# Cached keys loaded in small pieces and turned by VectorE, with ring slots of their own

## What is computed

```python
def sample_layer(x, c_fk, c_fv, c_logf, c_ckv, c_krope, c_mk, c_mv, p):   # x (8, 16, 1024)
    h = rmsnorm(x, p['g_mix'])
    fq, fk, fv, logf, q_lat, q_rope, ckv, krope, g_a, g_b = mixer_inputs(h, qpos, p)
    k_all = jnp.concatenate([c_fk, fk], axis=1)        # c_fk (8, 512, 8 heads, 64)
    v_all = jnp.concatenate([c_fv, fv], axis=1)
    ...
    fox_o = fox_attend(fq, k_all, v_all, cum[:, past:], cum, qpos, kpos)
    ckv_all = jnp.concatenate([c_ckv, ckv], axis=1)    # c_ckv (8, 512, 256), the latents
    ...
    mla_lat = mla_attend(q_lat, q_rope, ckv_all, krope_all, qpos, kpos)
    mix = mixer_output(fox_o, mla_lat, g_a, g_b, p)
    return residual_tail(x, mix, c_mk, c_mv, p), ...   # c_mk (8, 256, 4 heads, 128)

def fox_attend(q, k, v, cum_q, cum_k, qpos, kpos):
    s = jnp.einsum('bqhd,bkhd->bhqk', q, k) * FOX_SCALE
    ...                                                # forget-gate bias, mask, softmax, values

def cross_attend(h, mk, mv, p):
    q = (h @ p['w_xq']).reshape(B, T, X_HEADS, X_HEAD_DIM)
    s = jnp.einsum('bthd,bmhd->bhtm', q, mk) * X_SCALE
    ...                                                # softmax, values, w_xo

def residual_tail(x, mix, mk, mv, p):
    x = x + mix
    x = x + cross_attend(rmsnorm(x, p['g_x']), mk, mv, p)
    return x + moe(rmsnorm(x, p['g_ffn']), p)          # 32 experts, 4 per token
```

## Time and profile before

| | |
|---|---|
| median of 3 runs | 1525.36 us (1524.87 to 1526.36) |
| the profiled execution | 1524.94 us, of which the span from the first to the last instruction is 1523.1 us |
| TensorE busy | 1466.7 us, 96% of the span |
| VectorE, ScalarE busy | 552.6 us, 36%; 313.2 us, 21% |
| read from memory | 475.16 MB, 315 GB/s over the span |
| sample loop, about | 176 to 285 us |
| cross attention with memory loop, about | 502 to 568 us |
| experts, from about | 584 us |

### The profile page before, as it was taken

The page is one execution under the profiler, slowest core; times in us unless marked ns, Lnnn a source line. Parts: engine busy times, 40 slices in busy tenths (PEclk is TensorE's granted clock), DMA queues, the critical chain, the costliest instruction groups (busy, mean ns, idle before and its releaser), DMA issues.

```text
span 1523.1 us, 21869 instructions
## 1 busy us (share of the span) xinstructions
PE 1466.7 (96%) x8246; PEld 720.5 (47%) x8247; DVE 552.6 (36%) x1240; ACT 313.2 (21%) x676; POOL 45.4 (3%) x55
## 2 busy tenths in 40 slices
PE   8999899999999998999999999999999999999996
PEld 7766577655687653333333333333333333333332
DVE  4245444110302365333343333343333433333334
ACT  1225555210001441111111111111111111111111
POOL 0000000160000000000000000000000000000000
PEclk9999999999999998999999999999999999999998
DMA  9411466942332468999999999999999999999994
GB/s 287 131 67 47 116 184 215 304 156 86 111 125 83 153 259 360 427 427 429 428 428 429 430 428 428 428 430 389 431 428 428 429 429 429 428 429 429 429 428 199
DMA packets 83037, 483.48 MB, mean 317 GB/s; under 512 B 18144, under 2 KB 46080, under 8 KB 56368
## 3 DMA queue, kind: packets, MB, share of 16 engines
q1 hardware_dynamic: 68800, 471.78, 75.7%
q0 software_dynamic: 3168, 9.11, 2.6%
q10 hardware_dynamic: 11024, 1.96, 0.8%
HBM read 475.16 MB, written 4.65 MB: 315 GB/s over the span
## 4 chain that ended last, share of the span: by engine, by line
PE 79%; DMA 16%; DVE 2%; ACT 1%; issue 1%; SPq 0%; DVEq 0%; ACTq 0%
PE bank L529 74%; DMA ring<-in_w_gu 16%; PE bank L1283 1%; PE bank L683 1%; PE bank L1203 1%; DMA ring<-in_w_in 1%; PE bank L920 0%; PE bank L806 0%; PE bank L694 0%; PE bank L1066 0%; DVE small L1666 0%; PE bank L543 0%; DVE ring L1677 0%; PE bank L961 0%; DVE xr L1987 0%
## 5 line engine op out<-in xcount | busy, mean ns | idle before, releaser
L529 PE MATMUL bank<-ring,hT 128*64 128x512 f32 (+3 forms) x3648 | 814.1, 567 | 14.8 <-DMA ring<-in_w_gu 13.9
L529 PEld LDWEIGHTS bank<-ring,hT 128*64 128x64 f32 (+1 forms) x3648 | 305.6, 145 | 438.7 <-issue 387.8
L1945 DVE SCALAR_TENSOR_TENSOR xr<-bank,probTs,xr 128x512 f32<-128x512 f32 x198 | 139.2, 745 | 231.1 <-PE bank L529 231.1
L529 PE MATMUL bank<-hT,ring 128*128 128x384 f32 x384 | 124.4, 487 | 0.0
L2334 ACT ACTIVATE probTs<-hT 128x512 f32<-128x512 f32 x33 | 20.8, 629 | 412.4 <-DVE hT L1964 412.4
L1982 DVE TENSOR_TENSOR mlaT<-bank,foxT 128x512 f32<-128x512 f32 x33 | 22.8, 692 | 224.6 <-ACT foxT L2340 224.6
L529 PEld LDWEIGHTS bank<-hT,ring 128*128 128x128 f32 x384 | 72.9, 190 | 50.2 <-issue 0.2
L529 PE MATMUL bank<-ring 128*128 128x256 f32 (+7 forms) x434 | 84.9, 396 | 3.8 <-issue 2.5
L529 PE MATMUL bank<-foxT 64*128 64x512 bf16 x600 | 82.2, 380 | 0.8 <-ACT foxT L2340 0.8
L529 PEld LDWEIGHTS bank<-ring 128*128 128x128 f32 (+3 forms) x434 | 59.0, 171 | 20.0 <-issue 11.5
L2340 ACT CAST foxT<-bank 128x512 bf16<-128x512 f32 x33 | 19.3, 585 | 215.7 <-PE bank L529 215.7
(11 more groups left out here) (330 smaller groups left out, 1270.8 us busy)
## 6 DMA issues: line engine op xcount, KB each, us to landing
ring<-in_w_gu SPq DMA_DIRECT2D x128, 2048.0 KB, 24.1
ring<-in_w_down SPq DMA_DIRECT2D x64, 2048.0 KB, 26.5
ring<-in_w_in SPq DMA_DIRECT2D x16, 1024.0 KB, 11.5
ring<-in_cache_fox_k SPq DMA_DIRECT2D x8, 1024.0 KB, 4.8
ring<-in_cache_fox_v SPq DMA_DIRECT2D x8, 1024.0 KB, 7.7
ring<-in_cache_mla_ckv SPq DMA_DIRECT2D x8, 512.0 KB, 5.6
ring<-in_w_out SPq DMA_DIRECT2D x4, 1024.0 KB, 5.1
ring<-in_cache_mem_k SPq DMA_DIRECT2D x8, 512.0 KB, 3.2
```

The source lines that it names most:

```text
L529: return pe.matmul(o, l, r, start=start, stop=stop, skip_group_check=True)
L1945: v.scalar_tensor_tensor(x, sums[i % 2][:, :], gate_e[:, i // 2, e], x, ALU.mult, ALU.add).then_inc(shares_added, 1)
```

## The change

Fox keys of the batches in `FINE` (0, 1, 2, 3, 4 and 6) and all memory keys are loaded so that a 32x32 block transpose on VectorE finishes the turn. A row of keys is cut into pieces of 32 floats (128 bytes), and blocks of 32 tokens are laid on the 32 partitions where their channels will stand: 16 DMAs per fox key tile, each of 512 pieces, and 16 per memory tile, each of 256, plus one for the values, whose tokens are laid out in another order to match. VectorE waits for the tile and turns it from slot to `skT` in four transposes of 128x512 (`keys_in`), or to `xkT` in one of 128x1024 (`mem_out`). For batch 0 the four stand in the rounds i = 3 to 6 of the prompt's units (`KEYS_AT`), instead of two copies in round 7. TensorE's transposes and the copies out of banks on both engines go away for these tiles; batches 5 and 7 stay as they were. TensorE's first transposes of latents move ahead of the values in a step.

The ring's slots are shared out: two for fox keys, two for values, four for latents, by the batch's number, and the order of the stream is written anew. A slot with fine keys is released when VectorE has turned them (`keys_turned`).

```diff
+FINE = (0, 1, 2, 3, 4, 6)
...
-        for b in range(NB):
-            tile(("sk", b), whole(KT, FW, d["cache_fox_k"][0, b].rearrange("(p k) h n -> p k (h n)", k=KT)))
+        def key_tile(b):
+            if b not in FINE:
...
+            src = d["cache_fox_k"][0, b].rearrange("(i r) (g e) (f c) -> g e f r i c", r=32, e=2, c=32)
+            parts = []
+            for g in range(4):
+                for j in range(4):
+                    parts.append((lambda s, g=g, j=j: ring[32 * j:32 * j + 32, s, FW * g:FW * g + FW].rearrange("p (i c) -> p i c", c=32),
+                                  src[g, j // 2, j % 2, :, :, :]))
+            tile(("sk", b), parts)
...
+        for b in range(2):
+            key_tile(b)
+        for b in range(2):
+            latent_tile(b)
+        value_tile(0)
+        latent_tile(2)
+        key_tile(2)
+        latent_tile(3)
+        value_tile(1)
+        for b in range(NB - 2):
+            if b + 3 < NB:
+                key_tile(b + 3)
+            value_tile(b + 2)
+            if b + 4 < NB:
+                latent_tile(b + 4)
...
-            tile(("cm", b), [(lambda s: kview(s, 2, FW), d["cache_mem_k"][0, b].rearrange("(p k) h n -> p k (h n)", k=2)),
...
+            src = d["cache_mem_k"][0, b].rearrange("(i r) h (j c) -> h j r i c", r=32, c=32)
+            parts = []
+            for h in range(XH):
+                for j in range(4):
+                    parts.append((lambda s, h=h, j=j: ring[32 * j:32 * j + 32, s, MEM * h:MEM * h + MEM].rearrange("p (i c) -> p i c", c=32),
+                                  src[h, j, :, :, :]))
+            parts.append((lambda s: ring[:, s, 1024:2048].rearrange("p (k n) -> p k n", k=2),
+                          d["cache_mem_v"][0, b].rearrange("(k p) h n -> p k (h n)", k=2)))
+            tile(("cm", b), parts)
...
+        fl = place["fl"]
+        SK_AT, SV_AT, SC_AT = (fl, fl + 1), (fl + 4, fl + 7), (fl + 2, fl + 3, fl + 5, fl + 6)
...
             def turn_keys(b, pairs):
+                if b in FINE:
+                    return
...
-                for g in range(4):
-                    pe.wait_ge(free(("skT", b, g)), count(("skT", b, g)))
+                if b in FINE:
+                    pe.wait_ge(keys_turned, FINE.index(b) + 1)
...
                 if b + 1 < NB:
                     turn_keys(b + 1, (0, 1))
+                    turn_latents(b + 1, (0,))
                 if b >= 1:
                     sample_values(2 * b - 2)
                 if b + 1 < NB:
                     turn_keys(b + 1, (2, 3))
-                    turn_latents(b + 1)
+                    turn_latents(b + 1, (1,))
...
             def mem_scores(b):
-                for hh in range(2):
-                    pe.wait_ge(free(("cK", b, hh)), count(("cK", b, hh)))
+                pe.wait_ge(mem_turned, b + 1)
...
-                if n >= NRING:
-                    g = last_group[stream[n - NRING][0]]
+                last = slot_before[n]
+                if last and last[0] == "sk" and last[1] in FINE:
+                    sp.wait_ge(keys_turned, FINE.index(last[1]) + 1)
+                elif last:
+                    g = last_group[last]
                     sp.wait_ge(bank_full[g % 8], g // 8 + 1)
...
+            KEYS_AT = (3, 4, 5, 6)
+
+            def keys_in(b, pairs=(0, 1, 2, 3)):
+                if b in FINE:
+                    key = ("sk", b)
+                    dve.wait_ge(ring_loaded[slot(key)], loaded_at[place[key]])
+                    for g in pairs:
+                        last = v.transpose(skT[b % 2][:, g, :].rearrange("p (k i q) -> p i q k", k=KT, q=8), ring[:, slot(key), FW * g:FW * g + FW])
+                    if g == 3:
+                        last.then_inc(keys_turned, 1)
...
-                if i == 7:
-                    dve.wait_ge(fk_written, 32)
-                    for g in range(2):
-                        copy_out(("skT", 0, g), skT[0][:, g, :])
+                if i in KEYS_AT:
+                    if i == KEYS_AT[0]:
+                        dve.wait_ge(fk_written, 32)
+                    keys_in(0, (KEYS_AT.index(i),))
...
             def mem_out(b):
                 if b >= 2:
                     dve.wait_ge(full(("cS", b - 2)), count(("cS", b - 2)))
-                ps = take(("cK", b, 0))
-                give(v.tensor_copy(xkT[b % 2][:, 0:2, :], ps[:, :].rearrange("p (h s) -> p h s", h=2)), ("cK", b, 0))
+                key = ("cm", b)
+                dve.wait_ge(ring_loaded[slot(key)], loaded_at[place[key]])
+                v.transpose(xkT[b % 2].rearrange("p h s -> p (h s)"), ring[:, slot(key), 0:1024]).then_inc(mem_turned, 1)
```

More of the change, by code:

```diff
@@ L319, in build @@
         krope_ready = sem("krope_ready")
+        mem_turned = sem("mem_turned")
+        keys_turned = sem("keys_turned")
         ckv_ready = sem("ckv_ready")
@@ L450, in build @@
                     tile(("xo", j), whole(4, 512, d["w_xo"][0].rearrange("(k p) n -> p k n", p=P)[:, :, 512 * j:512 * j + 512]))
-            tile(("cm", b), [(lambda s: kview(s, 2, FW), d["cache_mem_k"][0, b].rearrange("(p k) h n -> p k (h n)", k=2)),
-                             (lambda s: ring[:, s, 1024:2048].rearrange("p (k n) -> p k n", k=2),
-                              d["cache_mem_v"][0, b].rearrange("(p k) h n -> p k (h n)", k=2))])
+            src = d["cache_mem_k"][0, b].rearrange("(i r) h (j c) -> h j r i c", r=32, c=32)
[7 more added lines that the diff above has]
+            tile(("cm", b), parts)
         place = {key: n for n, (key, _) in enumerate(stream)}
         NPRE = len(stream)
+        fl = place["fl"]
+        SK_AT, SV_AT, SC_AT = (fl, fl + 1), (fl + 4, fl + 7), (fl + 2, fl + 3, fl + 5, fl + 6)
         def slot(key):
-            return (place[key] - NPRE) % NRING
+            n = place[key]
+            if key[0] in ("sk", "sv"):
+                n = {"sk": SK_AT, "sv": SV_AT}[key[0]][key[1] % 2]
+            if key[0] == "sc":
+                n = SC_AT[key[1] % 4]
+            return (n - NPRE) % NRING
         loads = {}
         loaded_at = []
+        in_slot = {}
+        slot_before = []
         for key, parts in stream:
+            slot_before.append(in_slot.get(slot(key)))
+            in_slot[slot(key)] = key
             loads[slot(key)] = loads.get(slot(key), 0) + 16 * len(parts)
@@ L686, in turn_keys, with turn_latents @@
                     used_last(pe, i, ("sk", b))
-            def turn_latents(b):
+            def turn_latents(b, parts=(0, 1)):
                 s = arrived(pe, ("sc", b))
                 c3 = kview(s, KT, LORA)
-                for c in range(2):
+                for c in parts:
                     ps = open_bank(pe, ("scT", b, c))
@@ L695, in turn_latents @@
                     done(i, ("scT", b, c))
+                if 1 not in parts:
+                    return
                 ps = open_bank(pe, ("srT", b))
@@ L890, in sample_scores @@
                 lat = [qs[:, c, b, :, :].rearrange("p h q -> p (h q)") for c in range(2)]
-                for g in range(4):
-                    pe.wait_ge(free(("skT", b, g)), count(("skT", b, g)))
+                if b in FINE:
+                    pe.wait_ge(keys_turned, FINE.index(b) + 1)
+                else:
+                    for g in range(4):
+                        pe.wait_ge(free(("skT", b, g)), count(("skT", b, g)))
                 if b == 0:
@@ L1097, in mem_values @@
                 used_last(pe, i, ("cm", b))
-            mem_turn(0)
             for h in range(XH):
@@ L1686, in pipeline @@
                         part2(u0 + i - 1, units[i - 1])
+            KEYS_AT = (3, 4, 5, 6)
[7 more added lines that the diff above has]
+                        last.then_inc(keys_turned, 1)
+                else:
+                    for g in range(2):
+                        copy_out(("skT", b, g), skT[b % 2][:, g, :])
             for i in range(NU // 2 + 1):
@@ L1735, in cache_out @@
                     dve.wait_ge(full(("sS", 2 * b - 3)), count(("sS", 2 * b - 3)))
-                for g in range(2):
-                    copy_out(("skT", b, g), skT[b % 2][:, g, :])
+                keys_in(b)
                 copy_out(("scT", b, 0), scT[b % 2][:, 0, :])
@@ L2120, in keys_out @@
                     act.wait_ge(full(("sS", 2 * b - 3)), count(("sS", 2 * b - 3)))
-                for g in range(2, 4):
-                    copy_out(("skT", b, g), skT[b % 2][:, g, :])
+                if b not in FINE:
+                    for g in range(2, 4):
+                        copy_out(("skT", b, g), skT[b % 2][:, g, :])
             def latents_out(b):
@@ L2231, in _ @@
                 copy_out(("xq", h), xqT[:, h, :], TOK)
-            def mem_out(b):
-                if b >= 2:
-                    act.wait_ge(full(("cS", b - 2)), count(("cS", b - 2)))
-                ps = take(("cK", b, 1))
-                give(a.copy(xkT[b % 2][:, 2:4, :], ps[:, :].rearrange("p (h s) -> p h s", h=2)), ("cK", b, 1))
             def mem_exps(b):
```

23 lines of the change are left out of this document (3 added, 20 removed).

## The result

The changed kernel takes 1548.57 us (median of 1544.93 to 1552.87) against 1525.11 us before: ratio 1.0154, 95% interval 1.0126 to 1.0181. It is slower by 1.5%, where 1521.5 with a range to 1531 was forecast. The medians are 23.5 us apart. The profiled execution, the longest of the four, took 1552.87 us, span 1550.7, 27.6 us more than that of before; what follows accounts for these 27.6.

What follows compares the result with a forecast made beforehand. TensorE without gaps was taken to bound the stretch ahead of the experts, whose streaming starts when the routing table is ready. -7.6 + 0.2 - 1.2 + 5.2 = -3.4 us against 1524.94 gave 1521.5 us, range 1512 to 1531.

Steps and rivals of the forecast that it cites:

- What bounds the kernel: Whole kernel: the experts' weight streaming lasts as long as it lasts, so any gain arises ahead, shifting its start.
- Part 1: Sample loop: four steps each lose 1.89 us of TensorE's fox key turns, 7.6 us less; VectorE's transposes are covered.
- Step 0 and the units: Batch 1's turns in step 0: 0.2 us more; batch 0's among the prompt's attention units: 1.2 us less net.
- Part 3: Key tile loads: at 1000 pieces per us a tile takes 8 us against 18 of lead; cost nothing.
- Part 4: Memory stage: VectorE waits for 85 SP issues at 0.48 us each, so 5.2 us longer, not 5.7 shorter.
- Issues are dearer: Rival, SP between 508 and 556: issues cost 0.52 us and up; at 0.57 the total is 1529; chance 0.20.
- The clock: Granted clock: some 3 us to either side, as a memory stage with waits may get the lower level.
- Pieces move slowly: Rival, key and memory tile loads: 362 pieces per us, +25 us in sum, 1550; chance 0.06.

Runs made afterwards that it cites:

- odd_keys: Changed kernel, key tiles in 4 DMAs (batches 0, 1: 16, dense transposes), batch 1 turned early, fox pieces for batches 5, 7 instead of 4, 6: 1515.66 us, ratio 0.9931.
- no_spread: `mem_4_dmas` without GpSimd's six DMAs that spread the biases of batches 2 to 7 over the partitions: 1524.05 us, ratio 0.9983 to the kernel before.
- mem_4_dmas: Changed kernel with each memory tile's keys in 4 DMAs of 1024 pieces instead of 16 of 256: 1531.06 us, ratio 1.0036 to the kernel before.
- busy_waits: Changed kernel with extra matmuls of constants ahead of TensorE's waits for keys (sample batches 1, 6; memory batches 4 to 7): 1560.98 us, ratio 1.0233.
- dense_turns: `mem_4_dmas` with fox transposes written without output strides, so that part of the result isn't the reference's: 1530.11 us, ratio 1.0026 to the kernel before.
- turn_1_early: `mem_4_dmas` with VectorE's four transposes for batch 1 moved ahead of the first batch's maxima: 1531.03 us, ratio 1.0034 to the kernel before.

## Why the prediction was wrong

**What bounds the kernel: held.** The gain and the loss arise ahead of the experts, and from the routing table on both kernels take the same time within 0.6 us.

**Part 1, the loop's saving: about half of it was there.** A step that loses its key turns, and in which no tile was late, became 1.4 to 1.5 us shorter, not 1.9 (step 1 of `odd_keys` only 0.6, with the wait of 0.83 us in it): the latents' turns, now in two parts, take some of it back (0.60, 0.66 and 0.27 us in place of 1.04 and 0.27). The two steps that keep theirs became 0.4 to 0.6 longer (13.86 and 14.04 in `odd_keys`), with a wait of 0.32 us for ScalarE in each. So -7.6 should have been -3.9 even with every tile in time, as `odd_keys` shows. The price of a transpose, taken from "the copies' pace, 0.645 us each", was wrong as well: the change writes the output with strides, which the copies don't, and the transposes take 0.90 to 1.08. The diff shows these strides, and I weighed only the number of floats. The Trainium skill's "Vector Engine (DVE) Microarchitecture Reference", section 3.8, which I read as agreeing with 0.645, describes the array and not a strided output. The dense form took 0.62 in a row, near 0.645.

**Step 0 and the units: two wrong sizes.** Step 0 grew by 1.3, not 0.2, as four transposes take 3.68 and not 2.6. What the prediction called a place where TensorE "waits anyway" had little waiting: TensorE was busy for 8.88 of 9.40 us there before, and for 7.14 of 10.70 after. The turns taken from it became the wait of 3.62 us, and the clock of step 1 fell behind that. Among the units I let other work cover 0.8 of 2.6 us. The chain of the kernel after goes through all four transposes:

```profile
136.25 1.08 DVE ring L1738
...
143.57 0.98 DVE ring L1738
...
151.22 0.98 DVE ring L1738
...
159.50 0.98 DVE ring L1738
```

Together 4.0 us, less the 3.0 removed: +1.0, measured +1.1. Before, the chain of rounds 4 to 6 ran over TensorE; now it runs over VectorE in each of them, so the gaps that I had subtracted weren't there.

**Part 3, the lead of the key tiles: the step that failed.** "At 1000 pieces per us this holds with 8 us to spare", and so "Cost: nothing", had the right lead (the tile of batch 6 is issued from 230.97 and due at about 250), the right rate for pieces that are alone (943 per us), and the wrong assumption that they are. (By the prediction's own numbers, 18 less 8, the spare time was 10 us.) The spread of the biases was in the trace of before, one DMA of GpSimd in each step, and the prediction leaves it out. It holds half the engines for some 6 us, SP stands in the middle of a tile meanwhile, and what is behind it on SP stands too. A tile took SP 15 to 17 us, so that its last pieces came up to the next spread, and which tile met it was chance. `no_spread` shows it by taking the cause away.

Steps 1 to 6 lost 11.0 us instead of gaining 7.6. Of these 18.6 us the late tile of batch 6 has 10.0: 4.8 of wait (16.93 against 12.09 in `mem_4_dmas`) and 5.2 of clock behind it. The clock of step 1 has 4.9 (17.76 against 12.83 in `odd_keys`, where the wait of 0.83 us stands inside the step). The rest, 3.6, is the saving of part 1 that wasn't there.

**Part 4, memory keys: mechanism right, size short.** VectorE waiting for SP's issues, steps of some 8 us, no pause on TensorE's side but this one: as forecast. The 85 issues took 44.0 us from 522.08 to 566.09, 0.52 each with pauses, not 0.48 (+3.2). The last tile was there 3.4 us behind the end of its last issue (566.09 to 569.53), not 3 (+0.4), and the last scores ran at the lower clock (+0.4). With 0.4 us of a later start and the 5.2 of the forecast that makes 9.6; measured 9.8. The rival *Issues are dearer* had its sign change at just this 0.52. That four DMAs in place of 16 would bring the gain was open to me from the earlier trace rows, where 1024 pieces cost 0.57 and not four times 0.46; I used that row as an upper bound only. The rule of the Trainium skill ("DMA: Bandwidth & Descriptors", Rules for kernel authors) to join small transfers was the right advice against the change; that page's 0.95 us for 64 KB was not the price here, where a fox key DMA of 64 KB took SP 0.53 us from start to start.

**The clock: right cause, wrong place and size.** I gave it 3 us to either side, for the memory stage. By `busy_waits` it cost 5.8 in step 1 and 5.2 in step 6, and about 4 behind the memory stage (22.60 less 18.70): some 15 of the 27.6 us. Each of these stretches came behind waits of TensorE of 3.6 us or more, which the sum should have priced with the wait. Shorter ones did it too: behind 2.43 us in `dense_turns` and 2.58 in `turn_1_early` the eight matmuls of the scores took 1.93 and 1.94 us; behind 0.82 the clock stayed at 1.00. Length alone doesn't settle it: in the memory stage the scores behind a wait of 3.62 us (553.99) still ran at 1.00.

No rival held these parts together. *Pieces move slowly* had the cause of the late key tile, a rate that falls against another queue (362 per us in the earlier trace rows, 290 in the kernel after). Its 23.4 us for the memory stage, at 11.8 us a tile, didn't come: VectorE's turns were 8.0 to 8.8 us apart there. That its 1550 is the measured time is luck.

## What to carry to other kernels

A transfer has to be timed in the company that it will have: find every other queue's DMA in the stretch where it will run, the small ones too, and ask how many engines that one holds. A wait of TensorE costs its length and then, often, the pace of the work behind it (here 5.8 and 5.2 us behind waits of 3.62 and 4.75), so a change that makes short waits must be charged for both; and work taken from an engine that isn't idle shortens nothing if what replaces it comes later. Where loads set a stage's pace, speeding up an engine shows as a wait further on; cut many small DMAs into few with more pieces each, and space them out, before counting any gain on the engines.

## What the runs showed of the hardware

- A VectorE transpose of 128x512 floats takes 0.70 us alone and 0.62 in a row with a dense output; 1.07 and 0.92 to 0.95 with an output that steps as "p i q k" here. One of 128x1024 with a dense output takes 1.25.
- An SP DMA of 256 pieces of 128 bytes costs SP 0.49 us from start to start, one of 512 pieces 0.53, when nothing holds it up; four of 1024 cost 2.8 us when little is ahead in the queue and 5.0 to 7.2 when more pieces are. What SP's instruction waits for in the longer ones, no trace shows.
- A spread of 64 packets of 5 KB inside SBUF, 320 KB in some 6 us, held 47.7% of the engines' time and lowered the packets of the other queue from 943 to 290 per us.
- In the sample loop TensorE's scores ran at the lower clock behind every wait for key tiles or turns (2.43 to 5.62 us), and at 1.00 behind a wait that matmuls of constants filled. In the memory stage one wait of 3.62 us left the clock at 1.00.
